# Moving the matmul operands of an fp32 network kernel by 32 bytes in the on-chip memory

## The reference

```
def swiglu(x, w_gate, w_up, w_down):
    return (jax.nn.silu(x @ w_gate) * (x @ w_up)) @ w_down     # 1024 -> 2816 -> 1024, six times
x = x + 0.5 * rmsnorm(swiglu(rmsnorm(x, g_pre), w1_gate, w1_up, w1_down), g_post)
```

## The kernel before

| operand | before |
|---|---|
| `HH`, `HL` (with `PH`, `PL` in them) | 0 |
| ring slots 0 to 3, slot 9, slot 10 | 0 |
| `ar`, and all in it: `HIDH`, `HIDL`, `TH`, `TL`, `NH`, `NL`, `CH`, `CL`, `OHa` and its like, and slots 4 to 8 | 64 |

## Time and profile before

### The profile page before, as it was taken

The page is one execution under the profiler, slowest core; times in us unless marked ns, Lnnn a source line. Parts: engine busy times, 40 slices in busy tenths (PEclk is TensorE's granted clock), DMA queues, the critical chain, the costliest instruction groups (busy, mean ns, idle before and its releaser), DMA issues.

```text
span 3337.3 us, 51827 instructions
## 1 busy us (share of the span) xinstructions
PE 3229.6 (97%) x19480; PEld 2729.8 (82%) x19487; DVE 2059.6 (62%) x2673; ACT 1359.2 (41%) x2335; POOL 1345.4 (40%) x643
## 2 busy tenths in 40 slices
PE   8999999999999999999999999998999999999998
PEld 7998775789877899877579987765789987879986
DVE  7774444586647876354477765678477734477753
ACT  5553225344435445322444543324435521254542
POOL 6320562554116541065164404656553107635300
PEclk9999999999999999999999999999999999999999
DMA  4543221255332454322035533221145433215532
GB/s 156 159 143 104 90 87 32 70 152 151 114 123 83 138 160 120 105 83 87 19 99 153 153 117 108 101 68 34 51 135 166 123 103 108 82 57 146 168 104 95
DMA packets 99977, 362.59 MB, mean 109 GB/s; under 512 B 11088, under 2 KB 11344, under 8 KB 99536
## 3 DMA queue, kind: packets, MB, share of 16 engines
q1 hardware_dynamic: 88704, 320.90, 29.4%
q0 software_dynamic: 7776, 28.32, 5.1%
q10 hardware_dynamic: 3312, 10.86, 0.9%
HBM read 355.84 MB, written 4.19 MB: 108 GB/s over the span
## 4 chain that ended last, share of the span: by engine, by line
PE 73%; DVE 10%; issue 6%; ACT 4%; POOL 3%; DMA 3%; DVEq 0%; ACTq 0%; POOLq 0%; SPq 0%
PE psC L749 4%; PE psC L751 4%; PE psC L750 4%; PE psA L749 4%; PE psA L751 4%; PE psA L750 4%; PE psD L899 2%; PE psD L900 2%; PE psD L901 2%; PE psB L899 2%; PE psB L900 2%; PE psB L901 2%; DVE WL L2240 2%; DMA Y<-in_ws 2%; PE psB L984 2%
## 5 line engine op out<-in xcount | busy, mean ns | idle before, releaser
L629 POOL TENSOR_TENSOR WH<-raw,scalars 128x1024 fp32r<-128x1024 f32 (+1 forms) x194 | 377.8, 1948 | 1206.5 <-DMA raw<-in_w 1143.3
L2240 DVE TENSOR_TENSOR WL<-raw,WH 128x1024 fp32r<-128x1024 f32 x324 | 447.9, 1385 | 70.5 <-POOL raw L663 39.8
L631 POOL TENSOR_TENSOR WL<-raw,WH 128x1024 fp32r<-128x1024 f32 (+1 forms) x194 | 471.2, 2429 | 15.2
L1697 ACT ACTIVATE WH<-raw 128x1024 fp32r<-128x1024 f32 x324 | 340.4, 1053 | 48.9 <-DMA raw<-in_ws 37.2
L2316 DVE TENSOR_TENSOR WL<-raw,WH 128x1024 fp32r<-128x1024 f32 (+1 forms) x144 | 163.1, 1135 | 307.4 <-ACT WH L1718 305.8
L658 POOL TENSOR_TENSOR raw<-raw,Y 128x1024 f32<-128x1024 f32 x54 | 133.4, 2471 | 509.6 <-DMA raw<-in_ws 509.6
L1718 ACT ACTIVATE WH<-raw 128x1024 fp32r<-128x1024 f32 (+1 forms) x144 | 141.9, 989 | 375.7 <-DMA raw<-in_w 375.7
L749 PE MATMUL psA<-HH,WH 128*128 128x512 f32 x560 | 230.0, 411 | 0.0
L751 PE MATMUL psA<-HL,WH 128*128 128x512 f32 x560 | 218.5, 390 | 0.0
L750 PE MATMUL psA<-HH,WL 128*128 128x512 f32 x560 | 218.3, 390 | 0.0
L899 PE MATMUL psD<-TH,WH 128*128 128x256 f32 x720 | 202.0, 281 | 6.2 <-DVE psC L2287 2.7
(11 more groups left out here) (540 smaller groups left out, 9631.1 us busy)
## 6 DMA issues: line engine op xcount, KB each, us to landing
raw<-in_w SPq DMA_DIRECT2D x338, 512.0 KB, 3.5
raw<-in_ws SPq DMA_DIRECT2D x216, 512.0 KB, 3.6
Y<-in_ws SPq DMA_DIRECT2D x54, 512.0 KB, 4.7
raw<-in_ws POOLq DMA_DIRECT2D x54, 512.0 KB, 5.4
X<-in_x ACTq DMA_DIRECT2D x4, 512.0 KB, 9.5
NRAW<-in_mem ACTq DMA_DIRECT2D x2, 1024.0 KB, 7.2
out<-Y SPq DMA_DIRECT2D x8, 256.0 KB, 2.1
POSI<-in_pos ACTq DMA_DIRECT2D x4, 256.0 KB, 2.6
```

The costliest lines, as they stand in the source:

```text
L629: pool.tensor_tensor(WH[j][:, 0:w], raw[j][:, 0:w], zero[:, 0:1].broadcast_to([P, w]), ALU.subtract).then_inc(w_hi, 1)
L631: pool.tensor_tensor(WL[j][:, 0:w], raw[j][:, 0:w], WH[j][:, 0:w], ALU.subtract).then_inc(w_split, 1)
L1697: act.activation(WH[slots[i]][:], DX if i == 6 else raw[slots[i]][:], ACT.Copy).then_inc(part_hi, 1)
L2240: dve.tensor_tensor(WL[slots[i]][:], DX if i == 6 else raw[slots[i]][:], WH[slots[i]][:], ALU.subtract).then_inc(part_lo, 1)
```

## The change

The high and low halves of the residual begin 32 bytes later, the ring and all behind it 128 bytes later (so that its residue stays what it was), and the activation region begins 160 bytes later. Nothing else is touched: no instruction, order, wait, size or transfer changes.

```diff
--- before.py
+++ after.py
@@ -148,7 +148,9 @@
 
     KB = 1024
     X = sb("X", [P, KD, S])
+    region(32)
     HHo, HLo = region(16 * KB), region(16 * KB)
+    region(96)
     HH = sb("HH", [P, KD, S], F32R, offset=HHo)
     HL = sb("HL", [P, KD, S], F32R, offset=HLo)
     slot_at = [region(8 * KB) for _ in range(RING)]
@@ -176,6 +178,7 @@
     stat = sb("stat", [P, 8, 4])
     top8 = sb("top8", [P, QB, 8])
     WIT = sb("WIT", [P, QB, IDXH], offset=RYo)
+    region(-at[0] % 128 + 96 - 128)
     ar = region(88 * KB)
     slot_at += [ar + 72 * KB, ar + 80 * KB, ar + 28 * KB, ar + 36 * KB, ar + 64 * KB, SQo, Yo + 8 * KB]
     raw = [sb(f"raw{j}", [P, TILES * P], offset=o) for j, o in enumerate(slot_at)]
```

## The result

The changed kernel takes 3365.29 us (median of 2 runs, 3365.01 to 3365.57) against 3335.15 before: 30 us more, a ratio of 1.0091 with a 95% interval of 1.0074 to 1.0107. It is slower, by less than 2%. The span of its profiled execution is 3364.4 us, 27.1 more than before.

What follows compares the result with a forecast made beforehand. The prediction took TensorE's cost per matmul as the bound. Class terms +8 - 16 - 13 + 14 = -7 us gave 3330 from the profiled span and 3328 from the median, hence 3329 us; range 3284 to 3382.

Steps and rivals of the forecast that it cites:

- the two relations: Data and weights at equal residues of 128 bytes, or 64 apart: 226.5 against 228.7 to 233.3 ns; 120 against 113.3.
- A: Matmuls on `HH`, `HL` with 512 columns, about 3700: +2.2 ns each, +8 us; bounds 0 and +25 us.
- B: Matmuls on `HIDH`, `HIDL` and kin with 512 columns, about 3500: -4.5 ns each, -16 us; bounds -23 us and 0.
- C: Products 0, 3 and 5, 256 columns, 3888 matmuls: -3.3 ns each, -13 us; bounds -26 us and 0.
- D: Products 1, 2, 6 and 264 narrow down-projection matmuls, about 4150: +3.3 ns each, +14 us; bounds 0 and +28 us.
- E: Product 4, 1296 matmuls: no change, since both operands move together by 32 bytes.
- Nothing changes at all: Rival: residues are not the cause, levels come from tile order or what ran before; 3335 us within 3; chance 0.13.
- any offset serves: Rival: a quarter is as good as the better relation of each width; 3286 us; chance 0.09.
- Free of conflict: Rival: a quarter is better than all the trace shows; 3238 us, 2.9% less; chance 0.10.
- Collision all the way: Rival: moving reads run into the bytes of the weight load beside them; 3435 us, 3.0% more; chance 0.05.

Runs made afterwards that it cites:

- map2: Kernel of matmul triples only, network left out, halves spaced as in the kernel before, data moved 0 to 992 bytes; 226.7 to 234.4 ns (512 columns), 113.3 to 120.0 (256).
- ar192_b: Against the kernel before, only the activation region moved, by 128 bytes, from 192 to 64 after its weights modulo 256; 3336.41 us, ratio 1.0002.
- all32: Against the kernel before, everything begins 32 bytes later, each distance between data and weights kept; 3339.06 us, ratio 1.0009.
- hh32: Against the kernel before, only the halves of the residual moved, to byte 32; the activation region stayed at 64; 3351.44 us, ratio 1.0051.
- ar96: Against the kernel before, only the activation region moved, from byte 64 to 96; the residual halves stayed at 0; 3349.5 us, ratio 1.0048.
- both maps: `map2` and an earlier triples-only kernel that varied the bytes of 128 of data and weights; the earlier gave 233.3 ns at 0/0 with 512 columns.
- hh64: Against the kernel before, only the halves of the residual moved, to byte 64, which is 192 after the ring modulo 256; 3355.29 us, ratio 1.0063.
- ar0: Against the kernel before, only the activation region moved, to byte 0, so all data and weights begin alike; 3337.31 us, ratio 1.0004.

## Why the prediction was right or wrong

The forecast was -6 us, the result +30; the sign was wrong. The time lies in the range only because the range held both signs.

**What bounds the kernel, the classes and their counts** held, and so did the idea that the place of the data after its weights sets the cost. Of the 27.5 us, 24.5 lie in the named classes and 3.0 in the other matmuls, and in the named classes the stops are shorter than before, not longer. The page of the changed kernel still has 5.4 us to landing for the transfers that GpSimd issues:

```profile
raw<-in_ws POOLq DMA_DIRECT2D x54, 512.0 KB, 5.4
```

And among its waits, TensorE's in one bank of the pairs is 3.3 us where it was 5.8:

```profile
PE psA L902 <- DVE WL L2243: 3.3, 4, 0.8
```

The prediction's "at most 0.9 us" for such a wait holds for that bank alone. In another bank of the kernel before one lasted 1.3 us, which changes nothing in the sum:

```profile
PE psC L899 <- DVE WL L2240: 2.4, 6, 1.3
```

**The step that failed** is "I bound each class by the two relations that are shown, and take the middle, since 32 and 96 lie midway between 0 and 64 on the circle of 128". It is wrong twice. The circle has 256 bytes (`map2`, `ar192_b`), and on it the two relations were three points, 0, 64 and 192; the 228.7 of the earlier trace rows and the 233.3 of the earlier trace rows, which were averaged as one relation, are 64 and 192. The change went to 160 and 224, not to the middle between shown points. And between such points there is no slope: with 512 columns 0 costs 226.7 ns, and 32 costs 233.3, as much as 192. By class, level first and then sum:
- A: +2.2 ns forecast, +6.2 measured (227.9 to 234.1, just above its dearest level of 233.3). +20 us for +8.
- B: -4.5 ns forecast, 0 measured. -0.2 us for -16. This is the largest error of the four.
- C: -3.3 ns forecast, -1.2 measured (119.4 to 118.2). -6 us for -13.
- D: +3.3 ns forecast, +4.0 on its 3888 and +4.8 on the narrow ones. +9.5 us for +14, with 7.5 us less of stops in this execution than in the one before; by the levels alone it is +17.
- E: 0 forecast, +0.7 ns measured, +0.8 us. The plain matmuls of the attentions and the rest, taken as 0: +3.0 us, less than the 6.6 by which they differ between the kernel before and `all32`.

**The rivals.** *Nothing changes at all* and *any offset serves* fall with the result and with its parts `hh32` and `ar96`. But the doubt behind the first, raised by `NH` at 117.8 ns, pointed at something real: at 192 with 256 columns there are two levels at the same addresses. *Free of conflict* falls with both maps: no distance gave less than 226.7 and 113.3 at rest. *Collision all the way* had the right sign for A and D, but its price was read from a single distance (240 ns); A's mean is 234.1, and B did not rise at all. The criterion that I gave for it, A above 240, was not met. Its mechanism, reads that run into each other, was not tested.

**The rule against all of it.** That TensorE's reads never wait on anyone (the Trainium skill, "SBUF — State Buffer", section "Who interferes with whom") would have given no change. As far as other engines go the maps neither need nor contradict it: there nobody else was at work. But in `map2` the levels differ by up to 8 ns of 227 and 7 of 113 with nothing changed but the data's address. The measurement decides: one cost for each width, which the prediction drew from the rule, is not what this kernel has. Whether the two reads hold each other up is not shown.

## What to carry to other kernels

Where TensorE sets the time and matmuls run back to back with weight loads beside them, read the distance from start to start by tile before the duration: two tiles with the same shape and different levels can be a sign of address distance, worth 3 to 6% of a matmul here. Do not interpolate between two levels. A map of all offsets by itself is one short run, and it priced each class of this change to within 1 ns; where a distance has two rhythms it can miss, as by 4 ns in `hh64`. And judge by class, not by the total: `ar0` and `ar192_b` look like no change, and in each B fell by 20 or 13 us while D rose by 15 or 8.

## What the runs showed that I had not expected

- The cost of a triple of float32r matmuls depends on where its data stands from its weights modulo 256 bytes, in steps that follow no slope: 226.7 ns at 0, 233.3 at 32, 228.9 at 64 with 512 columns; 113.3 at 192, 117.3 at 160, 118.3 at 224 with 256 columns.
- The best distance of 512 columns (0, 226.7 ns) is with 96 the dearest of 256 columns in the same map (120 ns).
- At one and the same distance (192, 256 columns) two rhythms exist, 113.3 and 117.8 ns, each kept to the end of a stretch of 72 matmuls. Why the distance acts, which of the two reads holds up which, and what picks the rhythm stays open; only the effect was measured.
